# The start of a differential-attention layer: who issues one weight load, what the warm-up multiplies, and who rounds the first tile of x

## What is computed

```python
proj = u @ w_in                        # q | k | v | z, 2048 columns each
logits = einsum(q_blk, k) * scale + rel_bias      # causal mask
p = softmax(logits).reshape(B, DIFF_HEADS, 2, Q_BLOCK, S)
a = p[:, :, 0] - lam * p[:, :, 1]
o = rms_norm(einsum(a, v), subln_g) * (1.0 - lam_init)
y = (merge_blocks(o) * silu(z)) @ w_out
h = layer_norm(DN_ALPHA * x + y, g, b)
```

## Time and profile before

| | |
|---|---|
| median of three runs | 945.0 us (944.8 to 945.27) |
| the profiled execution | 945.5 us |
| its span, first to last instruction | 943.7 us |
| PE busy | 936.7 us (99% of the span) |
| DVE, ACT, POOL busy | 614.1, 324.5, 65.0 us |
| mean traffic of the DMA engines | 115 GB/s |

### The profile page before, as it was taken

The page is one execution under the profiler, slowest core; times in us unless marked ns, Lnnn a source line. Parts: engine busy times, 40 slices in busy tenths (PEclk is TensorE's granted clock), DMA queues, the critical chain, the costliest instruction groups (busy, mean ns, idle before and its releaser), DMA issues.

```text
span 943.7 us, 11713 instructions
## 1 busy us (share of the span) xinstructions
PE 936.7 (99%) x4212; PEld 779.4 (83%) x4212; DVE 614.1 (65%) x1191; ACT 324.5 (34%) x586; POOL 65.0 (7%) x140
## 2 busy tenths in 40 slices
PE   8999999999999999999999999999999999999998
PEld 7888888888888888888888888888888888888886
DVE  5545974687468746874687468746874799525465
ACT  4423433343334333332333233333333453222210
POOL 1200010001000100010001000100010000000032
PEclk9999999999999999999999999999999999999999
DMA  8722242215222422142214222522243222742433
GB/s 300 281 90 90 67 163 90 90 67 161 89 89 67 161 89 89 67 161 90 88 67 161 92 86 67 161 92 86 68 132 95 83 67 88 269 134 92 154 117 106
DMA packets 33799, 108.62 MB, mean 115 GB/s; under 512 B 4320, under 2 KB 6112, under 8 KB 33520
## 3 DMA queue, kind: packets, MB, share of 16 engines
q1 hardware_dynamic: 28320, 93.73, 29.6%
q0 software_dynamic: 2336, 9.48, 2.9%
q10 hardware_dynamic: 3120, 5.11, 1.6%
HBM read 104.07 MB, written 9.48 MB: 120 GB/s over the span
## 4 chain that ended last, share of the span: by engine, by line
PE 98%; DVE 1%; DMA 1%; SPq 0%; POOL 0%; ACT 0%; issue 0%
PE proj L959 79%; PE att L959 19%; DMA w_raw<-w_in_tiles_dram 1%; DVE big L952 0%; SPq L340 0%; DVE big L933 0%; POOL big L433 0%; DVE stats L888 0%; DVE w_split L819 0%; DVE big L885 0%; ACT w_split L555 0%; SPq L319 0%; DVE bias L939 0%; DVE mean_var L922 0%; DVE var_eps L924 0%
## 5 line engine op out<-in xcount | busy, mean ns | idle before, releaser
L959 PE MATMUL proj<-w_split,xg_split 128*128 128x512 f32 x1680 | 385.2, 389 | 0.0
L959 PEld LDWEIGHTS proj<-w_split,xg_split 128*128 128x128 f32 x1680 | 314.8, 188 | 65.2
L959 PE MATMUL proj<-xg_split,w_split 128*128 128x512 f32 x1536 | 353.2, 390 | 0.0
L959 PEld LDWEIGHTS proj<-xg_split,w_split 128*128 128x128 f32 x1536 | 287.6, 188 | 59.1
L450 ACT ACTIVATE w_split<-w_raw 128x1024 fp32r<-128x1024 f32 x128 | 135.9, 1061 | 349.2 <-PE proj L959 321.5
L644 DVE TENSOR_TENSOR w_split<-w_raw,w_split 128x1024 fp32r<-128x1024 f32 x128 | 155.8, 1223 | 119.3 <-ACT w_split L450 117.6
L722 DVE STREAM_TRANSPOSE scratch<-scratch 32x192 f32<-32x192 f32 (+2 forms) x384 | 141.8, 369 | 5.2
L959 PE MATMUL att<-w_split,xg_split 128*128 128x512 f32 x432 | 100.1, 389 | 1.4 <-DVE w_split L819 1.4
L959 PEld LDWEIGHTS att<-w_split,xg_split 128*128 128x128 f32 x432 | 80.9, 188 | 18.6 <-DVE w_split L819 1.8
L896 DVE TENSOR_TENSOR w_split<-w_raw,w_split 128x1024 fp32r<-128x1024 f32 x25 | 30.4, 1223 | 50.7 <-ACT w_split L608 50.7
L420 POOL TENSOR_SCALAR mean_sq<-sq_sum 128x1 f32<-128x1 f32 x32 | 10.3, 322 | 709.9 <-ACT scratch L502 708.5
(11 more groups left out here) (106 smaller groups left out, 469.7 us busy)
## 6 DMA issues: line engine op xcount, KB each, us to landing
w_raw<-w_in_tiles_dram SPq DMA_DIRECT2D x126, 512.0 KB, 3.3
w_raw<-w_out_tiles_dram SPq DMA_DIRECT2D x32, 512.0 KB, 3.4
bias_by_distance<-bias_lines POOLq DMA_DIRECT2D x8, 640.0 KB, 5.1
bias<-bias_by_distance POOLq DMA_DIRECT2D x8, 512.0 KB, 4.2
x_res<-in_x_dram ACTq DMA_DIRECT2D x4, 1024.0 KB, 5.6
big<-x_cols_dram SPq DMA_DIRECT2D x7, 512.0 KB, 8.8
out_dram<-big SPq DMA_DIRECT2D x12, 256.0 KB, 2.5
scratch<-in_ln_g_dram SPq DMA_DIRECT2D x1, 1024.0 KB, 7.8
```

The lines of the kernel that those rows point to most:

```text
L959: return nc.tensor.matmul(dst, lhsT, rhs, start=start, stop=stop, skip_group_check=True)
```

## The change

SP no longer issues SECOND of tile 0. ACT does, after it has waited for PE's third warm-up product, and ahead of everything else that it does; SP's later DMAs move up by one. The warm-up multiplies a constant of ones that is in memory from the start, so PE no longer waits for DVE, DVE no longer writes `ident`, and POOL no longer waits for PE before it does. Of x's first tile ACT rounds the first 256 columns and DVE the other 256, and PE and DVE's subtraction wait for both.

```diff
@@ SP
             for c in range(2):
                 sp.dma_start(w_raw[:, 0, FIRST[c]], w_in_tiles[0:P, FIRST[c]]).then_inc(first_loaded[c], 16)
-            sp.dma_start(w_raw[:, 0, SECOND], w_in_tiles[0:P, SECOND]).then_inc(raw_loaded[0], 16)
             load_x(1)
@@ POOL
             pool.wait_ge(consts_ready, 1)
-            pool.wait_ge(quarter_done, 1)
             nc.gpsimd.memset(ident[:], 0.0).then_inc(ident_zero, 1)
@@ ACT
-            xT_split(0)
+            act.wait_ge(warm_third, 1)
+            act.dma_start(w_raw[:, 0, SECOND], w_in_tiles[0:P, SECOND]).then_inc(raw_loaded[0], 16)
+            act.wait_ge(x_loaded[0], 16)
+            nc.scalar.activation(xg_split[:, 0, 0, 0:SEQ // 2], x_raw[:, 0, 0:SEQ // 2], ACT.Copy).then_inc(xT_hi, 1)
             act.wait_ge(first_loaded[1], 16)
@@ DVE
-            nc.vector.memset(ident[:], 1.0).then_inc(ones_ready, 1)
             dve.sem_inc(vz_moved, ST)
+            dve.wait_ge(x_loaded[0], 16)
+            nc.vector.tensor_copy(xg_split[:, 0, 0, SEQ // 2:], x_raw[:, 0, SEQ // 2:]).then_inc(first_x_hi, 1)
             dve.wait_ge(first_loaded[0], 16)
             nc.vector.tensor_copy(w_split[:, 0, 0, FIRST[0]], w_raw[:, 0, FIRST[0]]).then_inc(first_q_hi, 1)
+            dve.wait_ge(first_x_hi, 1)
             xT_split(0)
@@ PE
                 if first:
                     pe.wait_ge(xT_hi, 1)
+                    pe.wait_ge(first_x_hi, 1)
@@ PE, warm-up
-            pe.wait_ge(ones_ready, 1)
+            warm = nc.const_aps.tensor(1.0, (P, P), F32)
             for i in range(WARM):
-                nc.tensor.matmul(att[:, 3, 0:P], ident[:], ident[:], start=True, stop=True)
+                last = nc.tensor.matmul(att[:, 3, 0:P], warm, warm, start=True, stop=True)
+                if i == 2:
+                    last.then_inc(warm_third, 1)
```

More of the change, by code:

```diff
@@ L185, in diff_layer @@
         out_stored = sem("out_stored")
-        ones_ready = sem("ones_ready")
+        first_x_hi = sem("first_x_hi")
+        warm_third = sem("warm_third")
         ident_zero = sem("ident_zero")
```

## The result

The changed kernel is slower: 946.04 us (median of 22 runs, 944.76 to 948.46) against 945.02 us (22 runs, 944.45 to 945.4), a ratio of 1.0016 with a 95% interval of 1.001 to 1.0022. The forecast was 944.4, a gain of 0.6; it came to a loss of 1.0.

The account below looks back on a forecast made before the run. PE bounds the kernel, waiting only for SECOND at the start. SECOND landing at 7.1 us restarts PE at 8.5 instead of 9.14, a gain of 0.6: 945.0 - 0.6 = 944.4 us, range 943.4 to 946.1.

Parts of the forecast that it names:

- The place and its size: PE's wait for SECOND before tile 0's v/z products: 1.36 us idle, at most about 1.4 us to win.
- Warm-up, table load, halves of x: Start of PE and ACT: warm-up 0.3 us earlier, table load ending at 4.1, first product at 4.6; 0.1 us charged.
- The second rival: ACT 1.4 us late behind the table load, or SECOND landing at 7.7 again: 945.0 to 945.3; chance 0.2.
- I take the point between, 7.1 us: SECOND's landing on ACT's queue put at 7.1 us, PE restarting at 8.5, gain 0.6 us.
- The bounds: SECOND's landing: 6.2 us without any lag, 8.5 with the old lag.
- a lag of about 1 us: Delay of some DMA engines assumed for SECOND's landing; in the trace before some were 2.4 us behind.
- the late end: SECOND landing near 8.5 us, if a slow packet holds up the whole DMA engine.
- the late landing: Slower by sharing: SECOND lands at 8.3 to 8.5, PE restarts at 9.7 to 9.9, 945.6 to 945.8; chance 0.15.
- The argument by a separate queue: SECOND on ACT's queue lands near 6.2 us if slow packets on SP's queue hold up only that queue.
- The fourth rival: PE's clock stays low through the first 24 products after idling behind the warm-up: 949 us; chance 0.05.
- an early SECOND is worth up to 1.3 us: PE would go from tile 0's q/k products straight to v/z, with 0.1 us charged for ACT's lateness: 943.7 us.
- slack of 2.9 us: Tile 2 is needed at 17.46 us, DVE's parts end near 14.5; a shift of up to 1.4 us fits.

Follow-up runs that it names:

- the kernel with the issue alone: Kernel before with only the issue of SECOND moved to ACT, behind PE's third warm-up product; ident warm-up, x whole on ACT: 946.51 us against 944.92.
- the hold: Kernel before with SP holding x tile 1 and all later DMAs back until the k weights of tile 0 have landed: 944.55 us against 944.98.
- the swapped kernel: Kernel before with two SP DMAs swapped, x tile 1 asked for ahead of SECOND: 945.0 us against 944.66.
- the first-product kernel: Changed kernel with ACT issuing SECOND behind the first warm-up product instead of the third: 945.24 us against 944.98.
- the held one: Changed kernel, ACT still issuing SECOND, with SP's x tile 1 and later DMAs held until k has landed: 945.22 us against 944.66.
- the kernel with ACT's issue at once: Changed kernel without ACT's wait for the third warm-up product, so SECOND is issued at 0.74 us: 944.93 us against 944.92.
- the held kernels: SP issues SECOND, later DMAs wait for k: in the kernel before, 944.55 us against 944.98; with constant warm-up and x halves kept, 944.37 against 944.66.
- table first: Changed kernel with a one-column activation ahead of ACT's wait, so the table load runs at the start: 946.02 us against 944.98.
- the seventh-product kernel: Changed kernel with ACT issuing SECOND behind the seventh warm-up product instead of the third: 951.03 us (five runs) against 944.66.

## Why the prediction was wrong, point by point

- **The place and its size: right.** All of the difference lies in the first 15 us; behind them PE waits only for the 0.8 us at the end that both kernels have. From SECOND's landing to PE's restart is 1.43 us again (8.59 to 10.02).
- **Warm-up, table load, halves of x: right.** PE starts at 0.77, ACT issues at 2.43 (2.4), the table load ends at 4.17 (4.1), PE's first product starts at 4.66 (4.6). They cost nothing that is seen at the medians (944.58 with SP issuing, and 946.02 with the table load at the start again), and there is no drain behind the table load: the first half of x starts 0.02 us after it. The second rival's mechanism falls; here the measurement decides against the drain of some 1380 ns that the Trainium skill (ScalarE: Activation LUTs, "What ACT_TABLE_LOAD costs") adds to the load, at least for a first load.
- **"I take the point between, 7.1 us": the step that failed.** The bounds were 6.2 and 8.5, and 7.1 isn't even their middle (7.35). I took a lag of about 1 us because the trace could not tell; SECOND landed at 8.59, a lag of 2.4. The choice between the ends decided the sign, and two rows spoke for the late end: the issue came 0.3 us later, and every one of SP's next transfers was issued 0.47 us earlier. I gave the late landing 0.15.
- **Why it is late.** The argument by a separate queue ("if a slow packet on SP's queue holds up only that queue, it is near 6.2") has fallen: issued at 4.13, SECOND landed behind what SP had issued at 4.01. Nearly all landings come in the order of issue, whoever issues (the exception is SECOND in the kernel with the issue alone, 0.56 us ahead of a transfer issued 0.14 before it), and SECOND took longer the more was in flight: from 3.3 us with the hold to 5.6 before, 6.2 after and 7.9 in the last place. The Trainium skill (DMA: Bandwidth & Descriptors, "Issuing engines are not separate DMA queues") says that DMAs of all issuers interleave on the same engines and that a second issuer saves only issue time; the traces agree, in that ACT's queue never brought SECOND in earlier than SP's did, unless it also issued it earlier. What stays open is which part of the move costs the microsecond. A later place in the line is hardly enough: the swapped kernel gave SECOND the same place and a later issue, and lost 0.34 us, within the interval. No run separates ACT's queue beside a busy SP from SP's next transfers coming 0.47 us earlier.
- **What I left out: k.** I moved SECOND beside q and k and priced only SECOND. k landed 1.0 us later. It is hidden while SECOND is later still; where SECOND was early (the first-product kernel, the held one) k took the gain back.
- **The fourth rival: right in kind, wrong in form.** I looked for a clock that rises late; it rose in time and fell again, behind the 1.93 us wait, where no gap was left to absorb anything: 1.6 us on twelve products in the trace, some 2 us in four of 22 runs. The late rise is real elsewhere: in the kernel with ACT's issue at once. It shows in the weight loads (330 against 188 ns), as I read it in the earlier trace rows, and not in the granted clock, which is 1.00 there.
- **The gain that was there.** I took it that an early SECOND is worth up to 1.3 us. Where it was early by 2.3 us (the held kernels) the medians gained 0.3 to 0.4, which is within the interval. In one of them PE then waited 0.53 us at tile 2, whose slack of 2.9 us I had reckoned for the old issue times. And the profiled execution of before, 945.5 us, lies above all 22 timed runs (945.4 at most): its gap of 1.36 us is larger than the usual one, which by the relation above is some 0.9 us (an estimate). Landings differ by half a microsecond and more between executions, and I took one as the rule.

What else stays open: why SP-issued transfers in this stretch are slow at all (233 to 328 GB/s at a share of 0.85 to 0.93). The mean clocks of 0.999, which occur in most kernels, before too, cost nothing: in the three profiled executions that have one (table first, swapped, the held kernel) the clock is 1.00 until PE's last product is done and falls only then, at the very end of the span.

## What to carry to other kernels

Don't move a load's issue to another engine in the hope that a second queue overtakes: here it passed one neighbour at most, and a neighbour issued ahead of it (k) landed later. So price the neighbours as well as the load itself. Where PE waits for the first pieces of data, fewer transfers in flight shortened the landing here more than any choice of issuer, until the piece that was held back became the next wait; in the time no gain clear of the interval came of it. An idle stretch of PE that grows can cost twice, by its length and by the clock behind it, and then only in some of the runs: look at single runs, not at the median alone.

## What the runs showed of the hardware

- A transfer of 256 KB took from issue to landing 2.8 us as the first in line, 3.3 with three transfers ahead of it and none behind until k had landed, 4.9 to 5.6 with SP's next ones behind it (three executions), 7.9 as the ninth in line.
- Issued at the same moment from two engines, two transfers of 256 KB took 3.8 and 4.0 us to landing, where the first of them, issued first by SP and without the other, took 2.8.
- PE's granted clock fell from full to its level of 1.2 GHz (0.50 over 3.4 us in the seventh-product kernel, 0.57 over 4 us in the changed one) behind idle stretches of 1.90, 1.93 and 2.23 us, and came back while PE worked. Behind the 1.36 us of the kernel before it stayed full.
- The slow first products (weight loads of 330 against 188 ns) stand at a granted clock of 1.00 in the rows, in the warm-up and, with ACT's issue at once, up to about 9 us.
- The first ACT_TABLE_LOAD cost 1.28 us wherever it stood, and the next activation followed within 0.02 us wherever its data were in (six kernels).
